# Second layer's value products in two passes instead of three, with the softmax sums taken from the exponential

## Chip, cores and metric

One core of a Trainium2 chip runs the whole program. The metric is device time in microseconds (us), the median of several runs. The profile is of one further execution, in which every instruction was recorded.

## The reference, cut to what matters

The reference is one step of a two-layer encoder over 512 new frames of one stream (the prompt) and 64 frames of a running stream with 256 cached frames (the sample). The first layer has differential attention, the second "forgetting" attention. Each layer ends with a gated feed-forward network. The change lies in the second layer's attention alone, with 16 heads of 64 columns:

```python
s = einsum('bqhd,bkhd->bhqk', q, k) * 64 ** -0.5
s = s + cq - ck                                   # forget terms of query and key
p = softmax(where(k_pos <= q_pos, s, -inf))
o = einsum('bhqk,bkhd->bqhd', p, v)
```

All inputs are float32, and the products need float32's precision.

## The kernel before, in words

**Split products.** TensorE's fast format for 4-byte numbers (F32R) keeps fewer bits than float32. So every operand is split into a high part (the number copied to that format by ScalarE) and a low part (the rest, by VectorE or GpSimd), and a product is made as high x high + high x low + low x high: three passes of matmuls into one PSUM tile. `slice_` (L583) does that for all weights: six matmuls of 288 columns for one slice of 128 rows.

**Slots.** The second layer works in 8 groups of 2 heads. A group's projections (K, Q and V) are 3 units of 8 slices, 24 slots. `fox_attention` of PE (L786) puts the attention of group a between the projection slices of group a + 1. For the last group the slices are those of the output projection (`wo`, L862). Each engine has a program of its own, written out for all slots, and a table gives the slot at which each operation stands (L73 to L83: F_SCORE, F_MAX, F_EXP and so on; slots above 23 lie in the next group). Each engine works its list in order, and semaphores hold it where an operand isn't ready.

**One head.** For each of 5 jobs (jj; the sample's is first, then the prompt's four blocks of 128 queries from the longest, of 512 keys, to the shortest, of 128), PE makes the scores in `sps` (L669), VectorE adds the mask and takes the row's extreme (`row_max`, L1545), ScalarE takes the exponential (`exps`, L1059), PE transposes it into `tps` (L689), ScalarE copies the high part to `pth` or `pts` (`take_p`, L1079) and VectorE makes the low part `ptl` (`p_lo`, L1591), which frees `tps` for the next transposes. The next job's transposes wait for that.

**Value products and division.** The weights of the value product are 128 columns wide: 64 of V's high part and 64 of ones (`vh2`), or 64 of V's low part and 64 of zeros (`vl2`). So the output `ops` holds the product in one half of its partitions and the softmax's sum, repeated 64 times, in the other. `pv_sample` (L721) makes 6 matmuls (3 key blocks; one of 128 and one of 64 columns each), `pv_prompt` (L741) 12 (blocks of 512, 384, 256 and 128 columns, 3 passes each). `recip` (L1108) and `log_sample` (L1100) take the logarithm of the sums and exp(-x) of it on ScalarE into `rec`, `scale_o` (L1611) multiplies on VectorE, and `fox_o_hi` (L1116) and `fox_o_lo` (L1618) split the result for the output projection. `ops` is one tile: the next value product or V transposition waits until `scale_o` has read it.

**SP's queue.** SP issues all transfers in order (L491 to L525): a weight unit in each 8 slots (slot 6 of 8), the copies of K and Q between partition halves (`copy_k`, `copy_q`), loads of cached K and V, and stores of new K and V.

Of the kernel before, what the change touches and what calls it, by code (L numbers as in the profile page):

```python
# [12 lines left out]
P = 128  # L13
# [5 lines left out]
TQ = SEQ + P  # L19
# [59 lines left out]
F_K, F_Q, F_V = (9, 17, 24)  # L79
F_K_HI, F_K_LO, F_AUG = (11, 23), (14, 24), (17, 21)  # L80
F_Q_HI, F_Q_LO = (20, 21)
F_W_LO, F_SPLIT = (3, 1)
F_DUP_K, F_DUP_Q = (15, 25), 21  # L83
# [3 lines left out]
NORM_AT = 2  # L87
MASK_AT, MASK_COLS = 3 * P, 6 * P
# [55 lines left out]
def encoder(nc, w_units, w_forget, x_in, small, cst, cst16, rope_tab, k_past, v_past, f_past,  # L144
# [3 lines left out]
    with ExitStack() as ctx:  # L148
# [86 lines left out]
        vh2 = place("vh2", [P, 7, 4, 64], F32R)  # L235
        vl2 = place("vl2", [P, 7, 4, 64], F32R)
# [123 lines left out]
        den_logs = sem("den_logs")  # L360
# [20 lines left out]
        def v_parts(L, v, v2):  # L381
# [3 lines left out]
            return ((v2[:, 0:4, 0:4:3, :], tps.rearrange("p b (h n) -> p b h n", h=2)),  # L385
                    (v2[:, 4, 0:4:3, :], ops[:, 0:P].rearrange("p (h n) -> p h n", h=2)),
                    (v2[:, 5:7, 0:4:3, :], v_raw.rearrange("p b (h n) -> p b h n", h=2)))
# [12 lines left out]

        block = ctx.enter_context(nc.Block())
# [3 lines left out]
        def _(sp):  # L405
# [67 lines left out]

            def copy_q(g):
# [16 lines left out]
            def second_layer():  # L491
# [13 lines left out]
                for t in range(SLOTS * G + WO_ALL):  # L505
# [11 lines left out]
                    for a in range(G):  # L517
                        for h in range(2):
                            if t - SLOTS * a == F_DUP_K[h]:
                                copy_k(a, h)  # L520
# [61 lines left out]
        def _(pe):  # L582
# [134 lines left out]
            def head_cols(v, blk, h):  # L717

                return v[:, blk, 2 * h:2 * h + 2, :].rearrange("p x n -> p (x n)")

            def pv_sample(L, a, h):  # L721
# [3 lines left out]
                if L == FOX:  # L725
                    if some(a * 2 + h):
                        pe.wait_ge(o_scaled, val(a * 2 + h))
                    if a.c == 0 and h == 0:
                        pe.wait_ge(fox_set, 4)
                elif later(a):  # L730
                    pe.wait_ge(oln_done, val(a))
                hi, lo = (vh, vl) if L == DIFF else (vh2, vl2)
                wide, narrow = (hi, 2 * NEW), (lo, NEW)
# [1246 lines left out]
```

## Time and profile before

| | |
|---|---|
| median of 3 runs | 1491.17 us (1490.64 to 1492.05) |
| the profiled execution | 1489.46 us |
| its span, first to last instruction | 1487.6 us |
| PE busy | 1457.0 us, 98% |
| DVE busy | 592.3 us, 40% |
| ACT busy | 620.7 us, 42% |
| POOL busy | 445.7 us, 30% |
| transfers | 135.04 MB, mean 91 GB/s |

PE is TensorE, DVE VectorE, ACT ScalarE, POOL GpSimd, SPq the queue of the sync engine. Matmuls overlap one another, so what a matmul costs is read from the start of one to the start of the next rather than from its duration. The second layer's attention runs from about 760 to 1023 us of the span.

### The profile page before, as it was taken

What the parts mean: (1) busy time and instruction counts of PE and PEld (TensorE: products, weight loads), DVE (VectorE), ACT (ScalarE), POOL (GpSimd) and SP (SyncE); (2) the same over time, 40 slices, a digit from 0 to 9 for tenths busy, and PEclk for the clock granted to TensorE, in tenths of its full rate; (3) what the DMA queues carried; (4) which work ended last, traced back from release to release, by engine and by line L of the source; (5) the groups of instructions that cost most, each with busy time, mean ns of one, the idle gap of its engine ahead of it and who ended that gap; (6) DMA issues with size and microseconds to landing.
All of it is one profiled execution on the core that took longest, in us unless ns stands there. A gap on an engine that the chain in (4) does not pass through costs nothing.

```text
span 1487.6 us, 28062 instructions
## 1 busy us (share of the span) xinstructions
PE 1457.0 (98%) x10763; PEld 1417.0 (95%) x10763; DVE 592.3 (40%) x1205; ACT 620.7 (42%) x1043; POOL 445.7 (30%) x221
## 2 busy tenths in 40 slices
PE   7999999999999999999989999999999999999997
PEld 7889989999999999999989999999999999999997
DVE  6788777441111111111266666663511111111113
ACT  5566666442222222222246767764522222222121
POOL 0000001344444444433500000013444444444332
PEclk9999999999999999999999999999999999999999
DMA  5333333222222222222333343332222222222322
GB/s 192 120 103 104 105 101 91 72 71 85 85 79 77 84 85 82 79 92 78 110 110 88 87 115 100 99 84 71 71 85 85 82 76 82 85 81 79 87 84 89
DMA packets 48763, 135.04 MB, mean 91 GB/s; under 512 B 6752, under 2 KB 13280, under 8 KB 48688
## 3 DMA queue, kind: packets, MB, share of 16 engines
q1 hardware_dynamic: 48688, 134.02, 29.8%
q8 instruction: 49, 0.80, 0.2%
q14 instruction: 26, 0.21, 0.0%
HBM read 111.19 MB, written 11.83 MB: 83 GB/s over the span
## 4 chain that ended last, share of the span: by engine, by line
PE 88%; DVE 4%; ACT 3%; issue 2%; DMA 1%; POOL 1%; SPq 0%; DVEq 0%; ACTq 0%
PE ps L590 76%; PE ops L749 3%; PE tps L701 2%; PE sps L664 2%; PE ps L631 1%; ACT w_hi L957 1%; PE sps L687 1%; PE sps L681 1%; DVE qa L1541 1%; DVE pr L1560 1%; POOL w_lo L1344 0%; PE ops L756 0%; PE tps L714 0%; PE sps L827 0%; PE ops L737 0%
## 5 line engine op out<-in xcount | busy, mean ns | idle before, releaser
L1344 POOL TENSOR_TENSOR w_lo<-w_raw,w_hi 128x1024 fp32r<-128x1024 f32 (+1 forms) x159 | 373.6, 2350 | 1013.0 <-ACT w_hi L957 1011.5
L590 PE MATMUL ps<-xh,w_hi 128*128 128x288 f32 x2160 | 475.1, 301 | 10.1 <-issue 4.4
L590 PE MATMUL ps<-xh,w_lo 128*128 128x288 f32 x2160 | 462.8, 296 | 0.0
L590 PE MATMUL ps<-xl,w_hi 128*128 128x288 f32 x2160 | 462.4, 296 | 0.0
L957 ACT ACTIVATE w_hi<-w_raw 128x1024 fp32r<-128x1024 f32 (+1 forms) x199 | 207.6, 1043 | 447.0 <-PE ps L590 443.7
L590 PEld LDWEIGHTS ps<-xh,w_hi 128*128 128x128 f32 x2160 | 345.9, 189 | 20.6 <-issue 16.7
L590 PEld LDWEIGHTS ps<-xh,w_lo 128*128 128x128 f32 x2160 | 348.0, 189 | 0.0
L590 PEld LDWEIGHTS ps<-xl,w_hi 128*128 128x128 f32 x2160 | 348.0, 189 | 0.0
L590 PE MATMUL ps<-hh,w_hi 128*128 128x288 f32 x660 | 141.4, 294 | 0.0
L590 PE MATMUL ps<-hl,w_hi 128*128 128x288 f32 x660 | 140.4, 294 | 0.0
L590 PE MATMUL ps<-hh,w_lo 128*128 128x288 f32 x660 | 140.1, 293 | 0.0
L1464 DVE TENSOR_TENSOR uf<-ps,rs 128x576 f32<-128x576 f32 x44 | 33.3, 757 | 232.7 <-PE ps L590 232.7
L1859 DVE TENSOR_TENSOR hl<-hf,hh 128x576 f32 (+1 forms) x44 | 33.3, 758 | 228.7 <-ACT hh L1311 228.7
L1458 DVE TENSOR_TENSOR xT<-ps,xT 128x576 f32<-128x576 f32 (+1 forms) x43 | 32.5, 755 | 211.8 <-PE ps L590 211.5
L590 PEld LDWEIGHTS ps<-hl,w_hi 128*128 128x128 f32 x660 | 106.2, 187 | 0.0
L590 PEld LDWEIGHTS ps<-hh,w_lo 128*128 128x128 f32 x660 | 105.4, 188 | 0.0
L590 PEld LDWEIGHTS ps<-hh,w_hi 128*128 128x128 f32 x660 | 105.4, 188 | 0.0
L1311 ACT ACTIVATE hh<-hf 128x576 f32 (+1 forms) x44 | 30.2, 686 | 178.4 <-POOL hf L1400 178.4
L1560 DVE CUSTOM_DVE_ANT_0 pr<-sps,smalls 128x384 f32<-128x384 f32 (+3 forms) x160 | 75.3, 500 | 43.6 <-PE sps L687 24.1
L1599 DVE TENSOR_TENSOR ptl<-tps,pth 128x512 fp32r<-128x512 f32 (+1 forms) x96 | 47.0, 490 | 57.1 <-ACT pth L1091 56.8
L1400 POOL TENSOR_TENSOR hf<-sg,uf 128x576 f32<-128x576 f32 x44 | 62.8, 1428 | 0.0
L1065 ACT ACTIVATE pr<-pr,nmax 128x384 f32<-128x384 f32 (+3 forms) x80 | 45.0, 564 | 37.3 <-DVE nmax L1560 37.3
(211 smaller groups left out, 1705.8 us busy)
## 6 DMA issues: line engine op xcount, KB each, us to landing
w_raw<-w_units SPq DMA_DIRECT2D x184, 512.0 KB, 3.6
w_raw<-w_units SPq DMA_DIRECT2D x16, 384.0 KB, 3.0
qsw<-qsin SPq DMA_DIRECT2D x64, 72.0 KB, 2.0
ka<-ka SPq DMA_DIRECT2D x16, 224.0 KB, 4.5
xT<-x_in SPq DMA_DIRECT2D x8, 288.0 KB, 5.2
dk_out<-kf SPq DMA_DIRECT2D x8, 288.0 KB, 2.5
dv_out<-vf SPq DMA_DIRECT2D x8, 288.0 KB, 2.2
fk_out<-kf SPq DMA_DIRECT2D x8, 288.0 KB, 2.2
```

The source lines that it names most:

```text
L590: mm = nc.tensor.matmul(out[:, half, :], w[:, k, :], rhs[:, kt, half * HALF:(half + 1) * HALF], start=start and w is w_hi[slot] and rhs is ...
L749: mm = nc.tensor.matmul(ops[:, P * j:SEQ], w, p[:, j, P * j:SEQ], start=j == 0 and v is hi and p is pth, stop=j == 3 and v is lo)
L957: nc.scalar.activation(w_hi[slot][:, 0:kts, :], w_raw[slot][:, 0:kts, :], ACT.Copy).then_inc(w_hi_done, 1)
L1065: nc.scalar.activation(pr[:, slot, 0:width(i)], pr[:, slot, 0:width(i)], ACT.Exp, scale=-1.0, bias=nmax[:, slot:slot + 1], accum_out=den[: ...
L1311: nc.scalar.activation(at(hh, jt), hf[:], ACT.Copy).then_inc(hh_done, 1)
L1344: nc.gpsimd.tensor_tensor(w_lo[slot][:, 0:kts, :], w_raw[slot][:, 0:kts, :], w_hi[slot][:, 0:kts, :].bitcast(F32), ALU.subtract).then_inc( ...
L1400: nc.gpsimd.tensor_tensor(hf[:], sg[:], uf[:], ALU.mult).then_inc(hf_done, 1)
L1458: tt(halves(at(xT, k)), proj(n.c % 2), halves(at(xT, k)), ALU.add).then_inc(ps_read, 1)
L1464: tt(halves(dst), proj(n.c % 2) if src is None else src, halves(scale), ALU.mult).then_inc(ps_read, 1)
L1560: nc.vector.tensor_tensor_reduce(pr[:, slot, 0:width(i)], sps[:, jj % 2, 0:width(i)], mask[:, first:first + width(i)], -1.0, 3.0e38, ALU.a ...
L1599: tt(dst, src, hi.bitcast(F32), ALU.subtract).then_inc(pt_lo, 1)
L1859: tt(at(hl, jt), hf[:], at(hh, jt).bitcast(F32), ALU.subtract).then_inc(hl_done, 1)
```

## The change

V's high and low part now lie side by side in one tile `vv`, so that one matmul with the 128 columns [V high, V low] gives both products, one in each half of the partitions. Only the passes over P's high and P's low part are left. The ones are gone, and with them the sums. The exponential adds its row up (`accum_out`) into `dens`, and VectorE takes the reciprocal of five columns at a time (`make_share`). The result lies with queries across partitions, and it's needed with queries along the row, the same in 64 partitions. So one transfer writes it element by element to a row in HBM (`send_share`), and a second reads that row into 64 partitions (`fetch_share`). ScalarE copies the one half of `ops` to the partitions of the other (`move_prompt`, `move_sample`; before: logarithm, then exp), VectorE adds the halves (`join_o`) and multiplies by the fetched shares (`weigh_o`). The slot tables change in places. The two POOL memsets of ones and zeros go.

```diff
-F_SCORE, F_MAX, F_EXP = (3, 4, 5, 7, 7, 13, 13, 15, 18, 18), (1, 5, 5, 9, 9, 12, 14, 15, 18, 18), (2, 5, 6, 9, 9, 14, 14, 15, 18, 19)
-F_TURN, F_TAKE_P, F_P_LO = (5, 7, 9, 11, 13, 15, 17, 18, 21, 24), (5, 7, 9, 11, 13, 15, 16, 18, 21, 22), (6, 7, 9, 11, 12, 15, 16, 18, 21, 22)
-F_VT, F_TAKE_V, F_V_LO = (4, 1, 3)
-F_PVS, F_TAKE_S, F_SUM_S = (7, 17), (8, 19), (7, 19)
-F_PVP, F_SCALE_O, F_O_HI, F_O_LO = (15, 25), (16, 25), (17, 25), (17, 29)
-F_LN_S, F_RECIP = (10, 21), (15, 24)
+F_SCORE, F_MAX, F_EXP = (2, 5, 5, 7, 7, 13, 13, 15, 18, 18), (1, 5, 5, 7, 9, 13, 14, 15, 17, 18), (2, 5, 6, 8, 9, 13, 14, 15, 18, 18)
+F_TURN, F_TAKE_P, F_P_LO = (5, 7, 9, 12, 13, 15, 17, 18, 21, 24), (5, 8, 9, 10, 13, 15, 16, 18, 21, 22), (6, 7, 9, 9, 13, 15, 16, 18, 21, 22)
+F_VT, F_TAKE_V, F_V_LO = (3, 3, 3)
+F_PVS, F_TAKE_S, F_SUM_S = (9, 17), (9, 20), (9, 20)
+F_PVP, F_SCALE_O, F_O_HI, F_O_LO = (15, 25), (16, 25), (17, 28), (18, 28)
+F_LN_S, F_RECIP = (12, 21), (15, 25)
-F_DUP_K, F_DUP_Q = (15, 25), 21
+F_DUP_K, F_DUP_Q = (16, 25), 21
+F_SHARE, F_WEIGH, F_SEND, F_FETCH = (11, 20), (16, 27), (11, 18), (16, 24)
...
-        vh2 = place("vh2", [P, 7, 4, 64], F32R)
-        vl2 = place("vl2", [P, 7, 4, 64], F32R)
+        vv = place("vv", [P, 7, 4, 64], F32R)
+        share = place("share", [P, T])
+        dens = place("dens", [P, 2, 2, 8])
+        shares = place("shares", [P, 2, 2, 8])
...
+            def send_share(a, h):
+                sp.wait_ge(share_made, 2 * a + h + 1)
+                sp.dma_start(share_rows[2 * a + h].rearrange("(i p) -> p i", p=P), shares[:, a % 2, h, 0:5],
+                             allow_slow_non_contiguous=True).then_inc(share_out, 16)
+
+            def fetch_share(a, h):
+                sp.wait_ge(share_out, 16 * (2 * a + h + 1))
+                if a > 0:
+                    sp.wait_ge(o_joined, 2 * a + h - 1)
+                sp.dma_start(share[64 * h:64 * h + 64, :], share_rows[2 * a + h:2 * a + h + 1, 0:T].partition_broadcast(64)
+                             ).then_inc(share_in[h], 16)
...
                 if L == FOX:
                     if some(a * 2 + h):
                         pe.wait_ge(o_scaled, val(a * 2 + h))
-                    if a.c == 0 and h == 0:
-                        pe.wait_ge(fox_set, 4)
+                    for b in range(3):
+                        mm = nc.tensor.matmul(ops[:, 0:2 * NEW], head_cols(4 + b, h), pts[:, b, :], start=b == 0, stop=b == 2)
+                    mm.then_inc(pvs_done, 1)
+                    return
...
                 for j in range(4):
-                    for v, p in ((hi, pth), (hi, ptl), (lo, pth)):
+                    for v, p in ((vh, pth), (vh, ptl), (vl, pth)) if L == DIFF else ((vv, pth), (vv, ptl)):
...
                 else:
+                    if jj % 5 == 0 and a.c >= 2:
+                        act.wait_ge(share_made, 2 * (a.c - 2) + h + 1)
                     nc.scalar.activation(pr[:, slot, 0:width(i)], pr[:, slot, 0:width(i)], ACT.Exp, scale=-1.0,
-                                         bias=nmax[:, slot:slot + 1]).then_inc(exp_done, 1)
+                                         bias=nmax[:, slot:slot + 1], accum_out=dens[:, par, h, i:i + 1]
+                                         ).then_inc(exp_done, 1)
...
-            def recip(a, h):
+            def move_prompt(a, h):
                 act.wait_ge(pvp_done, G + i + 1)
-                nc.scalar.activation(rec[r, 0:SEQ], ops[o, :], ACT.Ln).then_inc(den_logs, 1)
-                act.wait_ge(den_logs, 2 * i + 2)
-                nc.scalar.activation(rec[r, :], rec[r, :], ACT.Exp, scale=-1.0).then_inc(rec_done, 1)
+                if a > 0:
+                    act.wait_ge(op_lo, i - 1)
+                nc.scalar.activation(rec[r, 0:SEQ], ops[o, :], ACT.Copy).then_inc(rec_done, 1)
...
-            def scale_o(a, h):
+            def join_o(a, h):
                 dve.wait_ge(rec_done, i + 1)
-                tt(rec[r, 0:SEQ], ops[r, :], rec[r, 0:SEQ], ALU.mult).then_inc(o_scaled, 1)
-                tt(rec[r, SEQ:T], osum[r, :], rec[r, SEQ:T], ALU.mult).then_inc(os_scaled, 1)
+                tt(rec[r, 0:SEQ], ops[r, :], rec[r, 0:SEQ], ALU.add).then_inc(o_scaled, 1)
+                dve.wait_ge(os_moved, i + 1)
+                tt(rec[r, SEQ:T], osum[r, :], rec[r, SEQ:T], ALU.add).then_inc(os_scaled, 1)
+
+            def weigh_o(a, h):
+                dve.wait_ge(share_in[h], 16 * (a + 1))
+                dve.wait_ge(o_scaled, i + 1)
+                dve.wait_ge(os_scaled, i + 1)
+                tt(rec[r, :], rec[r, :], share[r, :], ALU.mult).then_inc(o_joined, 1)
+
+            def make_share(a, par, h):
+                dve.wait_ge(exp_done, 10 * G + 10 * a + 5 * h + 5)
+                if a >= 2:
+                    dve.wait_ge(share_out, 16 * (2 * (a - 2) + h + 1))
+                nc.vector.reciprocal(shares[:, par, h, 0:5], dens[:, par, h, 0:5]).then_inc(share_made, 1)
...
-                for tile, value in ((vh2[:, :, 1:3, :], 1.0), (vl2[:, :, 1:3, :], 0.0)):
-                    nc.gpsimd.memset(tile.bitcast(F32), value).then_inc(fox_set, 2)
```

`fox_o_hi` waits for `o_joined` now. In SP's program `send_share` and `fetch_share` stand at their slots of the group, ahead of `copy_k` of the same slot. In VectorE's program `weigh_o` stands right behind `join_o` where both have slot 16.

## Rows read from the trace of the kernel before

**Rows 1.** The page, busy time of each engine.
```profile
PE 1457.0 (98%) x10763; PEld 1417.0 (95%) x10763; DVE 592.3 (40%) x1205; ACT 620.7 (42%) x1043; POOL 445.7 (30%) x221
```
**Rows 2.** Busy time by stretch: us, PE, PEld, DVE, ACT, POOL, clock, DMA, GB/s.
```profile
830.00:860.00 30.00, 29.58 (x218) 28.20 (x217) 20.92 (x49) 20.82 (x40) 2.40 (x1) 1.00 0.32 91
```
**Rows 3.** Waits, 750 to 1060 us: total us, times, longest.
```profile
PE tps L701 <- DVE vl L1589: 1.7, 7, 0.2
PE ops L749 <- DVE ptl L1599: 1.3, 7, 0.2
```
**Rows 4.** Timeline of PE, prompt value product: start, us, engine, line, operation.
```profile
780.25 0.40 PE L749 MATMUL ops<-pth,vh 128*128 128x512 f32 x1
...
782.10 0.39 PE L681 MATMUL sps<-ka,qa 128*128 128x384 f32 x1
```
**Rows 5.** Timeline of PE, sample value product of the third group.
```profile
835.91 0.31 PE L737 MATMUL ops<-pts,vh 128*128 128x128 f32 x1
836.05 0.24 PE L737 MATMUL ops<-pts,vl 128*128 128x64 f32 x1
836.13 0.30 PE L737 MATMUL ops<-pts,vh 128*128 128x128 f32 x1
...
836.61 0.48 PE L590 MATMUL ps<-xh,w_hi 128*128 128x288 f32 x2
```
**Rows 6.** Groups by line and form, ACT and DVE: busy us, mean ns | idle before.
```profile
L1065 ACT ACTIVATION_READ_ACCUMULATOR pr<-pr,nmax 128x1 f32 x80 | 15.0, 187 | 0.0
L1114 ACT ACTIVATE rec<-rec 64x576 f32<-64x576 f32 x16 | 10.9, 684 | 0.5
L1129 ACT ACTIVATE og<-ops 128x512 f32<-128x512 f32 x8 | 4.7, 592 | 1.1 <-PE ops L749 1.1
L1622 DVE TENSOR_TENSOR ol<-rec,oh 64x576 fp32r<-64x576 f32 x16 | 12.0, 752 | 1.4 <-ACT oh L1124 1.1
L1568 DVE RECIPROCAL rden<-den 128x1 f32<-128x1 f32 x40 | 6.3, 158 | 2.8 <-ACT pr L1065 2.8
```
**Rows 7.** Timeline of ACT, third group.
```profile
839.16 0.79 ACT L1069 ACTIVATE pr<-pr,nmax 128x256 f32<-128x256 f32 x2
...
846.53 0.59 ACT L1112 ACTIVATE rec<-ops 64x512 f32<-64x512 f32 x1 [1.46 <-PE ops L749]
...
849.40 0.60 ACT L1091 ACTIVATE pth<-tps 128x512 fp32r<-128x512 f32 x1 [0.70 <-PE tps L701]
...
852.85 0.80 ACT L1069 ACTIVATE pr<-pr,nmax 128x256 f32<-128x256 f32 x2
```
**Rows 8.** Timeline of DVE, third group.
```profile
848.50 0.67 DVE L1615 TENSOR_TENSOR rec<-ops,rec 64x512 f32<-64x512 f32 x1
849.10 0.21 DVE L1616 TENSOR_TENSOR rec<-osum,rec 64x64 f32<-64x64 f32 x1
850.03 0.69 DVE L1599 TENSOR_TENSOR ptl<-tps,pth 128x512 fp32r<-128x512 f32 x1 [0.72 <-ACT pth L1091]
...
853.33 1.22 DVE L1476 TENSOR_TENSOR w_lo<-w_raw,w_hi 128x1024 fp32r<-128x1024 f32 x1
```
**Rows 9.** Timeline of PE, the next transposes.
```profile
851.27 0.52 PE L701 MATMUL tps<-cstf,pr 128*128 128x128 f32 x3
```
**Rows 10.** DMA queue: packets, MB, share; then issues, KB each, us to landing.
```profile
q1 hardware_dynamic: 48688, 134.02, 29.8%
...
kf<-k_past SPq DMA_DIRECT2D x16, 128.0 KB, 3.5
...
half_sel<-cst SPq DMA_DIRECT2D x8, 1.0 KB, 2.8
...
lf_out<-lf SPq DMA_DIRECT2D x1, 36.0 KB, 1.6
```
**Rows 11.** Timeline of SP's queue, third group.
```profile
841.38 0.33 SPq L419 DMA_DIRECT2D w_raw<-w_units  x1
...
855.11 1.11 SPq L479 DMA_DIRECT2D qb<-qa  x2
```

More of the change, by code:

```diff
@@ L359, in encoder @@
         fox_set = sem("fox_set")
-        den_logs = sem("den_logs")
+        os_moved = sem("os_moved")
+        share_made = sem("share_made")
+        share_out = sem("share_out")
+        share_in = [sem(f"share_in{h}") for h in range(2)]
+        o_joined = sem("o_joined")
         rec_done = sem("rec_done")
@@ L378, in encoder, with v_parts @@
         y_done = sem("y_done")
-        def v_parts(L, v, v2):
+        def v_parts(L, v, low):
             if L == DIFF:
                 return ((v[:, 0:4, :], tps[:]), (v[:, 4, :], ops[:, 0:P]), (v[:, 5:7, :], v_raw[:]))
-            return ((v2[:, 0:4, 0:4:3, :], tps.rearrange("p b (h n) -> p b h n", h=2)),
-                    (v2[:, 4, 0:4:3, :], ops[:, 0:P].rearrange("p (h n) -> p h n", h=2)),
-                    (v2[:, 5:7, 0:4:3, :], v_raw.rearrange("p b (h n) -> p b h n", h=2)))
+            c = slice(1, 3) if low else slice(0, 4, 3)
+            return ((vv[:, 0:4, c, :], tps.rearrange("p b (h n) -> p b h n", h=2)),
+                    (vv[:, 4, c, :], ops[:, 0:P].rearrange("p (h n) -> p h n", h=2)),
+                    (vv[:, 5:7, c, :], v_raw.rearrange("p b (h n) -> p b h n", h=2)))
         def t_index(L, a, jj):
@@ L518, in second_layer @@
                         for h in range(2):
+                            if t - SLOTS * (a + 1) == F_SEND[h]:
+                                send_share(a, h)
+                            if t - SLOTS * (a + 1) == F_FETCH[h]:
+                                fetch_share(a, h)
                             if t - SLOTS * a == F_DUP_K[h]:
@@ L715, in transpose_v, with head_cols @@
                 nc.tensor.transpose(ops[:, 0:P], vf[:, SEQ:TQ], ident).then_inc(vt_done, 1)
[L717 to L719 removed]
+            def head_cols(blk, h):
+                return vv[:, blk, 2 * h:2 * h + 2, :].rearrange("p x n -> p (x n)")
             def pv_sample(L, a, h):
@@ L744, in pv_prompt @@
                 pe.wait_ge(os_taken, val(v_index(L, a, h) + 1))
-                hi, lo = (vh, vl) if L == DIFF else (vh2, vl2)
                 for j in range(4):
-                    for v, p in ((hi, pth), (hi, ptl), (lo, pth)):
-                        w = v[:, j, :] if L == DIFF else head_cols(v, j, h)
-                        mm = nc.tensor.matmul(ops[:, P * j:SEQ], w, p[:, j, P * j:SEQ],
-                                              start=j == 0 and v is hi and p is pth, stop=j == 3 and v is lo)
+                    for v, p in ((vh, pth), (vh, ptl), (vl, pth)) if L == DIFF else ((vv, pth), (vv, ptl)):
+                        w = v[:, j, :] if L == DIFF else head_cols(j, h)
+                        mm = nc.tensor.matmul(ops[:, P * j:SEQ], w, p[:, j, P * j:SEQ], start=j == 0 and v is not vl and p is pth,
+                                              stop=j == 3 and (v is vl or v is vv and p is ptl))
                 mm.then_inc(pvp_done, 1)
@@ L1053, in take_v @@
                     act.wait_ge(pvp_done, val(v_index(L, a, 0)))
-                for b, (dst, src) in enumerate(v_parts(L, vh, vh2)):
+                for b, (dst, src) in enumerate(v_parts(L, vh, False)):
                     if b == 2:
@@ L1704, in fox_attention @@
                         if s == F_SCALE_O[h]:
-                            scale_o(a, h)
+                            join_o(a, h)
+                        if s == F_WEIGH[h]:
+                            weigh_o(a, h)
+                        if s == F_SHARE[h]:
+                            make_share(a, par, h)
                         if s == F_O_LO[h]:
```

35 lines of the change are left out of this document (17 added, 18 removed).

## The prediction

> **What bounds the kernel.** I read the page's busy times first: PE is busy in 98% of the span and each other engine in under half [rows 1]. An average says nothing of one stage, so next the busy time of 30 us inside the second layer's attention, at the full granted clock (2.4 GHz): PE 29.58, DVE 20.92, ACT 20.82 us [rows 2]. Then who PE waits for there: the longest sums that a DVE operation causes are 1.7 and 1.3 us in all, each 7 waits of at most 0.2 us [rows 3]. So this stage is the length of PE's work, and DVE and ACT have a third of it spare, if what is added doesn't come at a wrong moment. Since PE is in order and dense, a matmul taken out is worth the distance from its start to the next one's start.
>
> **What PE loses: the prompt's third pass.** 12 matmuls of `pv_prompt` take from 780.25 to 782.10 us, where the next operation starts: 1.85 us [rows 4]. The three passes have the same shapes (512, 384, 256, 128 columns), so one is a third, 0.617 us. It goes for 2 heads of 8 groups, 16 times: 9.9 us.
>
> **The sample's product.** Six matmuls take from 835.91 to 836.61, 0.70 us; one of 128 columns is 0.14 before the next, the first one of 64 columns 0.08 [rows 5]. Three of 128 columns stay. At 0.14 each they take 0.42 and 0.28 us is saved; if each costs what the average of the six is (0.70 / 6 = 0.117), 0.35 us are saved; the lowest price in sight is the 0.08 of the small one, 0.24, which saves 0.46. I take the middle one: 16 x 0.35 = 5.6 us, with ends 4.5 and 7.4.
>
> The Trainium skill (TensorE: Matmul & The Clock Gate, section "Wait — 56ns, not 53.3ns?") has another price: a matmul costs its columns at 2.4 GHz and some 2.5 ns. By that the prompt's pass would be 0.54 us, and the sample's saving (576 columns before, 384 after) 0.09 us: 10.1 us in all. The prompt's row agrees within some 15%; the sample's doesn't, 0.70 us against 0.26 by the rule. Such a low gain is one of the rivals below, with the price of my rows.
>
> **ACT.** Out: the exp over 576 columns, 16 x 0.684 = 10.9 us. The logarithm (0.59 us) becomes a copy, and a copy of 512 columns out of `ops` takes the same 0.592 [rows 6, 7]. In: the reading of the accumulator behind each exponential, 0.187 us [rows 6], for 80 exponentials: 15.0 us. Together +4.1 us over 8 groups of some 32 us, 0.5 us a group. Cover: ACT's idle third [rows 2]. If it had none, it would be 4 us. More of interest is that each exponential is done 0.19 us later for the transposes; at present no transposition waits for an exponential (the waits that there are stand in [rows 3]), so I cost it at nothing.
>
> **DVE.** The two multiplications become two additions of the same shapes (0.67 and 0.21 us [rows 8]): nothing. In: one multiplication of 64x576 from SBUF, by the nearest row 0.752 us, and one reciprocal, 0.158 us for one column and hardly more for five [rows 6]. 16 x 0.91 = 14.6 us, nearly 2 us a group, from 20.9 to some 22.7 in 30 us. Again in idle time, provided the operands are there.
>
> **The tile `ops`** gets free earlier: product 0.6 us shorter, and no exp of 0.68 between the copy and DVE's operation. A gain only where PE waited for that; it doesn't [rows 3], so nothing. **POOL's** two memsets and PE's one wait for them go: nothing, as POOL has no part in the stage's end.
>
> **The way of the sums.** This is the only new wait on a shared engine, so I followed its times, on the third group's first head. The last two exponentials end at 839.16 + 0.79 = 839.95 [rows 7], with two reads of the accumulator 840.3; reciprocal 840.5. Then `send_share`: 640 separate elements of 4 bytes to HBM. No row shows such a transfer. The lower bound is the quickest landing, 1.6 us (`lf_out`). The nearest in size of its pieces is 2.8 us (16 rows of `half_sel`, 1 KB). The upper bound: all of the queue's packets, mostly of kilobytes, cost on average 0.298 x 1487.6 x 16 / 48688 = 0.146 us on one of 16 engines; 40 of them on each are 5.8 us, and with the 1.6 us 7.4 [rows 10]. I take 2.8: landed at 843.3. `fetch_share`, 64 rows and 147 KB out of HBM, is like the load of cached K, 3.5 us (lower bound 2.8): 846.8.
>
> When does DVE need it? ACT now starts on `ops` at 846.53 [rows 7], after the change 0.6 us sooner, 845.9; copy to 846.5, two additions of 0.67 and 0.21 and the hand-overs: 847.6. So the share is there 0.8 us before the multiplication can start, which then ends at 848.4. Behind it in DVE's list stands the low part of the next transposed block, which has to wait for ACT in any case: it starts at 850.03, behind a copy from 849.40 [rows 7, 8], 0.6 us sooner after the change, 849.4. So there is a further 1.0 us of cover; the share costs nothing up to a landing at 848.65, 1.85 us after my estimate. For the second head the table leaves 7 slots between reciprocal and multiplication instead of 5, and though DVE splits weights from 853.33 to 854.55, just ahead of the reciprocal [rows 8], it is the looser one of the two.
>
> **SP's queue.** Two waits come before other transfers. Behind `send_share` of the first head stand a store, the load of cached V and the weight unit of 841.38 [rows 11]; SP passes it at 840.5, so nothing is late for the weights. `fetch_share` holds `copy_k` up to some 843.3, which the next group's scores need, 10 slots (over 10 us) later. `send_share` of the second head waits until some 854.7, and the `copy_q` behind it waits for its own operand up to 855.11 anyway [rows 11]. `fetch_share` of the second head then holds one copy and a store for 2 or 3 us; a weight unit issued at slot 22 is first split 11 slots later. All costed at nothing; if the cover of a weight unit were gone, PE would wait for it in every group.
>
> **The sum.** Gain 9.9 + 5.6 = 15.5 us. Against it some small waits: PE is ahead of the others by nearly 1 us a group more, and the 14 waits of 3.0 us in sum [rows 3] may grow by half: 1.5 us. Net 14.0. The profiled execution took 1489.46 us around a span of 1487.6; it should come to some 1475.5. The median of the runs is 1.7 us above that execution, so 1491.2 - 14.0 = 1477.2. I give 1477.0.
>
> **Rivals.**
>
> 1. *Gain partly given back.* The 0.187 us behind each exponential and 2 us more of DVE a group delay low parts on which transposes wait. If half of the 80 reads came to stand in PE's way, 7.5 us are lost: 1484.5. The low gain (sample product saves the 0.09 or little more) without any waits gives 1491.2 - 9.9 - 1.4 = 1479.9, and with them up to 1486. For it: rows of 0.2 us waits show that some low parts are just in time. Against: none of these waits names an exponential. Chance 0.15 for 1480 to 1488.
>
> 2. *DVE stands at the multiplication for the share: slower.* Place: `weigh_o` of the first head, at slot 16; behind it the low part of the 512 block, without which the transposes of 851.27 [rows 9] don't start. It decides from a landing after 848.65. At the upper bound (send 7.4, fetch 3.5 us) the share lands at 840.5 + 10.9 = 851.4, 2.75 us late, 8 times: 22 us, less the 15.5: 1497.7. Even with before is at 1.9 us late. For it: two transfers one behind the other, the fetch standing behind a 512 KB weight unit and a store in the same queue, and 640 pieces. Against: even the sum of the nearest rows leaves 1.85 us. The Trainium skill (DMA: Bandwidth & Descriptors, section "Rules for kernel authors") speaks against this edit: a strided last dimension becomes one descriptor per element, and it advises to rearrange. It gives no price for 640 of them; if the rearranged pattern's 19-fold cost, given there for transposes by plain transfers, held for the 1.6 us, this would be far beyond the upper bound, and no row here shows it. Chance 0.08.
>
> 3. *No change.* The removed matmuls' time comes back as waits, since PE and the others go in step: about 1491. Against it the spare third [rows 2]. Chance 0.04.
>
> That the change doesn't do what it says: the sums could be read before they are complete or the pass could stay; the matmul count excludes the latter, and the former would change no time. No chance of its own.
>
> **Chances and range.** Forecast 0.73, for 1473 to 1480: ends from the sample term (4.5 to 7.4 instead of 5.6, prompt's third 0.58 to 0.65) and waits of 0 to 3 us. Rival 1 0.15, rival 2 0.08, rival 3 0.04. The range of 8 in 10 is the forecast's own, stretched into rival 1: 1473 to 1484. A measurement of this kernel tells differences from 0.2%, 3 us. Faster by more than that: forecast and rival 1, 0.88. Within: rival 3 and a little of 2, 0.05. Slower: 0.07.
>
> **What the changed profile would show.** PE has 3 x 16 + 4 x 16 = 112 matmuls less (10651), `pv_prompt` takes 1.23 us instead of 1.85, the sample's product 0.35 instead of 0.70. The waits of DVE name the share's transfer for at most a few us in all, and PE's waits stay under some 6 us in the stage. ACT gains 80 accumulator reads of 0.19 us. Wrong would be: a send that lands after 5 us or more, a multiplication in `weigh_o` with a DMA as releaser and over 1 us each time, PE idle before transposes in each group, or a stage whose PE work shrinks by under 12 us.

## The result, and the profile after

Slower by 8%: 1613.61 us is the median of the changed kernel (1612.60 to 1616.90, 4 runs), against 1490.91 us for the kernel before, measured beside it (4 runs). The ratio is 1.0829, 95% interval 1.0815 to 1.0842. The prediction said 1477.0 us, range 1473 to 1484. The profiled execution has a span of 1610.8 us.

The page, busy time of each engine and the granted clock in 40 slices; the first line answers to [rows 1]:

```profile
PE 1476.1 (92%) x10651; PEld 1435.4 (89%) x10651; DVE 607.3 (38%) x1237; ACT 616.5 (38%) x1107; POOL 443.0 (28%) x219
...
PEclk9999999999999999999889888888899999999999
```

PE has the 112 matmuls less that were foretold (10651), and yet it is busy 19.1 us longer than before. Its idle time, span less busy, went from 1487.6 - 1457.0 = 30.6 us to 134.7. So two things are to be explained: 104 us of waiting, and busy time that grew although work went. Who waits for what, in the list of waits over the whole run (total us, times, longest) for PE, DVE and SP's queue; the first line answers to the waits for a low part in [rows 3]:

```profile
PE tps L728 <- DVE ptl L1625: 74.3, 8, 9.8
PE sps L714 <- DMA qb<-qa: 26.1, 8, 4.9
...
DVE rec L1651 <- DMA share<-share_rows: 96.1, 16, 10.2
...
SPq L494 <- DMA share_rows<-shares: 129.6, 15, 10.3
```

DVE's multiplication in `weigh_o` stands for the share in all 16 heads, up to 10.2 us. PE's transposes wait for the low part behind it once in each of 8 groups, 9.3 us on average. A second wait, of 26.1 us, is for the copies of the new queries. Both lead back to SP's queue, shown here from the timeline (start us, duration, line, operation) for both heads of one group:

```profile
873.79 0.38 SPq L486 DMA_DIRECT2D share_rows<-shares  x1
874.22 0.52 SPq L448 DMA_DIRECT2D fk_out<-kf  x1
...
883.68 0.47 SPq L494 DMA_DIRECT2D share<-share_rows  x1
...
894.22 0.38 SPq L486 DMA_DIRECT2D share_rows<-shares  x1
894.65 1.43 SPq L502 DMA_DIRECT2D qb<-qa  x2
...
904.19 0.46 SPq L494 DMA_DIRECT2D share<-share_rows  x1
```

The fetch may only go out when the send has landed: 9.9 and 10.0 us after it here, 9.6 to 12.6 us over the 16 heads. My estimate was 2.8, my upper bound 7.4. What is issued behind the send lands late too: `fk_out` took 12.0 us (median) where it took 2.2.

The trace also shows what the DMA engines do in that time. For each of the 16 sends some 670 packets of 4 bytes start within the first 3 us, 7 ns each in the median. After that little moves until the send has landed (columns of [rows 2]):

```profile
877.80:883.60 5.80, 3.71 (x31) 3.56 (x29) 1.60 (x5) 2.79 (x6) 0.00 (x0) 1.00 0.43 25
```

That is 25 GB/s at a DMA share of 0.43, where the stretch in [rows 2] has 91 GB/s at 0.32: the packets of the other transfers last long and carry little. From 4 us after the issue to 1 us before the fetch it is 18 to 34 GB/s for each of the 16 sends. So the 10 us don't go into starting one piece after another; they pass between the start of the pieces and their landing.

DVE and PE at the end of this group's wait (timeline; in brackets the idle time before and its releaser); then two pairs of the same matmuls from an undisturbed stretch; then the busy time by stretch with the columns of [rows 2]:

```profile
889.26 0.75 DVE L1651 TENSOR_TENSOR rec<-rec,share 64x576 f32<-64x576 f32 x1 [9.71 <-DMA share<-share_rows]
889.93 0.67 DVE L1625 TENSOR_TENSOR ptl<-tps,pth 128x512 fp32r<-128x512 f32 x1
...
890.75 0.87 PE L728 MATMUL tps<-cstf,pr 128*128 128x128 f32 x3 [9.24 <-DVE ptl L1625]
...
892.39 0.68 PE L617 MATMUL ps<-xh,w_lo 128*128 128x288 f32 x2
892.87 0.68 PE L617 MATMUL ps<-xh,w_hi 128*128 128x288 f32 x2
```

```profile
779.56 0.43 PE L617 MATMUL ps<-xl,w_hi 128*128 128x288 f32 x2
779.83 0.42 PE L617 MATMUL ps<-xh,w_lo 128*128 128x288 f32 x2
```

```profile
836.00:848.00 12.00, 4.10 (x18) 4.13 (x19) 5.03 (x12) 4.34 (x10) 0.00 (x0) 0.58 0.33 73
...
884.00:910.00 26.00, 15.44 (x92) 14.53 (x92) 13.21 (x26) 11.03 (x23) 0.00 (x0) 0.80 0.68 102
...
891.00:893.00 2.00, 2.00 (x10) 2.00 (x10) 2.00 (x8) 1.83 (x6) 0.00 (x0) 0.50 0.02 4
```

After PE had stood for 9.24 us, two matmuls of 288 columns take 0.48 us from start to start, where the same pair took 0.27 us at 779.56. From 891 to 893 us the granted clock is 0.50, so 1.2 instead of 2.4 GHz, called the half clock below; over the two longer stretches its mean is 0.58 and 0.80. This is the busy time that grew: the removed products are worth 15.4 us (below), so 19.1 + 15.4 = 34.5 us were added. The trace lets it be counted in a second way. Over the whole run PE is busy for some 76 us while the granted clock is 0.50, in the kernel before for 3. Of the 0.48 us for a pair 0.21 are added by the low clock, and of the 73 us more at this clock the same share is 32 us, an estimate.

One group, from the first head's sample product to the same in the next group, takes 46 to 48 us instead of 32.1.

### The profile page after: what moved, and what is told of

The parts are those of the page before. It is cut to its first block, busy times and chain, and to the rows that moved or that the text cites. A ratio compares the mean times of both kernels' runs of the same rounds, so it can differ in the third digit from the quotient of the medians.

```text
span 1610.8 us, 28016 instructions
## 1 busy us (share of the span) xinstructions
PE 1476.1 (92%) x10651; PEld 1435.4 (89%) x10651; DVE 607.3 (38%) x1237; ACT 616.5 (38%) x1107; POOL 443.0 (28%) x219
## 4 chain that ended last, share of the span: by engine, by line
PE 75%; DMA 15%; DVE 4%; issue 2%; ACT 2%; POOL 1%; SPq 1%; DVEq 0%; ACTq 0%
PE ps L617 68%; DMA share_rows<-shares 8%; DMA share<-share_rows 3%; DMA qb<-qa 2%; PE tps L728 2%; PE sps L691 1%; PE ops L775 1%; PE ps L658 1%; DVE ptl L1625 1%; POOL w_lo L1372 0%; PE ops L782 0%; PE tps L741 0%; PE sps L853 0%; DVE pr L1586 0%; PE sps L714 0%
## 5 line engine op out<-in xcount | busy, mean ns | idle before, releaser
L617 PE MATMUL ps<-xh,w_hi 128*128 128x288 f32 x2160 | 485.0, 307 | 8.9 <-issue 3.9
L617 PE MATMUL ps<-xl,w_hi 128*128 128x288 f32 x2160 | 470.1, 300 | 0.0
L617 PE MATMUL ps<-xh,w_lo 128*128 128x288 f32 x2160 | 469.9, 300 | 0.0
L617 PEld LDWEIGHTS ps<-xh,w_hi 128*128 128x128 f32 x2160 | 354.5, 194 | 18.6 <-issue 16.6
L617 PEld LDWEIGHTS ps<-xl,w_hi 128*128 128x128 f32 x2160 | 355.9, 193 | 0.0
L617 PEld LDWEIGHTS ps<-xh,w_lo 128*128 128x128 f32 x2160 | 355.2, 193 | 0.0
L728 PE MATMUL tps<-cstf,pr 128*128 128x128 f32 x312 | 59.2, 293 | 78.7 <-DVE ptl L1625 74.3
L728 PEld LDWEIGHTS tps<-cstf,pr 128*128 128x128 f32 x312 | 39.2, 148 | 85.2 <-issue 75.2
```

What stands on the lines that cost most here:

```text
L617: mm = nc.tensor.matmul(out[:, half, :], w[:, k, :], rhs[:, kt, half * HALF:(half + 1) * HALF], start=start and w is w_hi[slot] and rhs is ...
L728: mm = nc.tensor.transpose(tps[:, b, :], pr[:, slot, P * b:P * b + P], ident)
```

## The experiments

"Before" is the kernel before, measured beside each experiment: 1490.4 to 1490.6 us each time. "Send to fetch" is the distance of the two issues on SP's queue. The fetch also has a slot of its own, so for quick sends this is an upper bound.

**1. No transfers.** The share tile is filled with ones by POOL, so the division is left out:

```diff
-                            if t - SLOTS * (a + 1) == F_SEND[h]:
-                                send_share(a, h)
-                            if t - SLOTS * (a + 1) == F_FETCH[h]:
-                                fetch_share(a, h)
+                nc.gpsimd.memset(share[:], 1.0).then_inc(share_set, 1)
```

> The changed kernel without both transfers: the multiplication takes a tile of ones set once, so the output isn't divided by the sums; exponential, reciprocal, moves and slot tables stay. Theory A (the transfers by way of HBM alone cost the 123 us, and the rest of the forecast stands): PE idle of the stage back to that of before, no stretch at the low clock, two-pass products worth 13 to 16 us: 1475 to 1480 us. Theory B (the accumulator reads, the extra VectorE work or the new slot tables also hold PE): between 1485 and 1560 us, with PE waits on ptl that don't name a transfer.

1481.1 us, ratio 0.9939 (0.9923 to 0.9956), 1 us above theory A's range. All else of the change is a gain; the way of the sums is the whole loss, 1613.6 - 1481.1 = 132.5 us. Added up over 16 heads, from first matmul to the next operation, the prompt products went from 30.54 to 20.48 us and the sample products from 11.16 to 5.86: 15.4 us (the 15.2 us in an expectation below is the same sum from rows rounded to 0.01 us). Of this 9.3 us arrive in the time. The largest wait that was added stands in the list:

```profile
PE ops L772 <- DVE ptl L1624: 4.0, 7, 0.6
```

**2. The send in 128 pieces of 20 bytes.** Each partition writes its five shares side by side, so they reach the tokens in another order:

```diff
-share_rows[2 * a + h].rearrange("(i p) -> p i", p=P), shares[:, a % 2, h, 0:5], allow_slow_non_contiguous=True
+share_rows[2 * a + h].rearrange("(p i) -> p i", p=P), shares[:, a % 2, h, 0:5]
```

> The send writes each partition's five values side by side, 128 pieces of 20 bytes instead of 640 of 4 (the shares come back in another order, so the output is wrong in its scaling). Theory A (the engines write small pieces to HBM one after the other, about 10 us / 40 = 0.25 us each): 8 pieces on an engine, landing in 2 to 4 us; the kernel within 1475 to 1500 us. Theory B (a write to HBM with a second transfer behind it is slow as such, whatever the pieces): still 8 to 10 us from send to fetch, and over 1580 us.

1490.81 us (one run); send to fetch 1.8 to 3.4 us. The form of the write is the cause of the 10 us, and not the way to HBM as such. But for the order in which the shares arrive nothing else differs from the change, so the form alone is worth 1613.6 - 1490.8 = 122.8 of the 132.5 us. The share is still late at times, and the whole gain of the products is gone again:

```profile
DVE rec L1651 <- DMA share<-share_rows: 15.5, 10, 3.4
```

**3. Fewer columns.** The send writes 5, 4, 3, 2, 1, 5, 3 and 1 columns in the eight groups, and the fetch reads a row of constants (no division):

```diff
+                n = (5, 4, 3, 2, 1, 5, 3, 1)[a]
-share_rows[2 * a + h].rearrange("(i p) -> p i", p=P), shares[:, a % 2, h, 0:5]
+share_rows[2 * a + h, 0:n * P].rearrange("(i p) -> p i", p=P), shares[:, a % 2, h, 0:n]
```

> Groups 0 to 7 send 5, 4, 3, 2, 1, 5, 3, 1 of the five columns (640, 512, 384, 256, 128, 640, 384, 128 pieces of 4 bytes); the fetch reads a constant row, so the output isn't the reference's. Theory A (a price by piece): the time from send to fetch is a straight line in the number of pieces, about 1.6 us + 0.21 us for each piece on an engine: 10, 8.3, 6.6, 5, 3.3, 10, 6.6, 3.3 us. Theory B (a fixed price for such a pattern, as in its preparation): 9 to 10 us for each group. Rival C (writes to neighbouring addresses hinder each other): not a line, steeper with more columns.

1599.5 us (one run). Send to fetch, first head: 10.9, 9.8, 9.6, 9.4, 8.4, 10.9, 9.6 and 8.1 us. A fifth of the pieces takes nearly as long as all. So a price per piece, on which my upper bound was built, is refuted. Theory B, one price for such a pattern, fits these numbers best; what about the pattern is dear is open until experiments 4 and 5. A column is 128 neighbouring words in HBM, and five columns take only 2 to 3 us longer than one.

**4. The same 640 pieces, written into SBUF** (again with constants fetched):

```diff
-share_rows[2 * a + h].rearrange("(i p) -> p i", p=P), shares[:, a % 2, h, 0:5]
+spread[:, 0:10:2], shares[:, a % 2, h, 0:5]
```

> The send's 640 pieces of 4 bytes go into SBUF (every second word of a small tile) instead of HBM, and the fetch reads a constant row of HBM; the output isn't the reference's. Theory A (it is the small write to HBM that is slow): 2 to 3.5 us from send to fetch, kernel at 1475 to 1495 us. Theory B (640 separate pieces are slow wherever they go, in making or moving them): 8 to 10 us and over 1580 us.

1492.46 us (one run); send to fetch 2.2 to 3.6 us. So 640 pieces of 4 bytes aren't slow as such; in HBM, side by side, they are.

**5. Eight forms of a write to HBM,** one per group, with constant data and no division:

```diff
+                n, step = ((5, 0), (1, 1), (1, 16), (1, 128), (16, 16), (8, 8), (2, 2), (1, 8))[a]
+                    dst = forms[2 * a + h, 0:P * step].rearrange("(p n) -> p n", n=step)[:, 0:n]
+                    sp.dma_start(dst, pieces[:, 0:n], allow_slow_non_contiguous=True).then_inc(share_out, 16)
```

> Edit: the send writes a constant tile in a form of its own in each of the 8 groups, and the fetch reads a constant row, so the division is left out. Forms by group: 640 pieces of 4 bytes as in the change; 128 pieces of 4 bytes side by side; 128 of 4 bytes each 64 bytes apart; 128 of 4 bytes each 512 bytes apart; 128 of 64 bytes side by side; 128 of 32 bytes side by side; 128 of 8 bytes side by side; 128 of 4 bytes each 32 bytes apart. Read as the time from send to fetch on the sync engine's queue. Theory A (writes of a few bytes that fall beside each other in HBM are made one after the other): about 9 to 10 us in the groups 0 and 1, 5 to 9 in group 6 (8 bytes), under 3.5 in groups 3, 4 and 5, and the spacing at which it falls tells the size of the stretch that is held. Theory B (each write of 4 bytes to HBM is slow, wherever it falls): 8 us or more in groups 1, 2, 3 and 7 alike, under 3.5 in 4 and 5.

1516.53 us (one run).

| pieces | send to fetch, us, heads 0 and 1 |
|---|---|
| 640 of 4 B, five columns, as in the change | 10.8, 11.7 |
| 128 of 4 B, side by side | 9.0, 7.9 |
| 128 of 4 B, 64 B apart | 1.9, 2.7 |
| 128 of 4 B, 512 B apart | 3.0, 2.3 |
| 128 of 64 B, side by side | 3.2, 2.2 |
| 128 of 32 B, side by side | 1.9, 2.2 |
| 128 of 8 B, side by side | 3.8, 4.3 |
| 128 of 4 B, 32 B apart | 3.2, 2.7 |

The timeline of SP's queue, second and third form:

```profile
847.02 0.33 SPq L493 DMA_DIRECT2D forms<-pieces  x1
...
854.88 0.49 SPq L503 DMA_DIRECT2D share<-cst  x1
...
872.00 0.33 SPq L493 DMA_DIRECT2D forms<-pieces  x1
...
873.88 0.49 SPq L503 DMA_DIRECT2D share<-cst  x1
```

The same 128 pieces of 4 bytes are about four times quicker when they lie 64 bytes apart, and 32 bytes are enough. Pieces of 8 bytes side by side take half as long as those of 4, less than the 5 to 9 us that I expected. So writes are slow when they start 4 bytes apart, half as slow at 8 bytes, and quick at 20 (experiment 2) and 32 bytes. No run has a distance between 8 and 20 bytes. The Trainium skill (DMA: Bandwidth & Descriptors, section "Specifications") says that below 512 B a transfer does a read-modify-write. That alone doesn't tell the slow forms here from the quick ones, since all pieces are below 512 B. If its read-modify-writes are what is made one after the other here, then only where pieces share such a stretch; no run here shows the mechanism itself.

**6. Slow send, late multiplication.** The first idea for a repair without touching the transfer (of the slot tables, here and below, only what changes is shown):

```diff
-F_O_HI, F_O_LO = (17, 28), (18, 28)
+F_O_HI, F_O_LO = (24, 36), (24, 36)
-F_WEIGH = (16, 27)
+F_WEIGH = (23, 35)
```

> Edit: the slow send stays as it is in the change; only the multiplication by the shares (and the products of osum after it) stand 7 to 8 slots later, some 7 us behind their old place. Theory A (most of the loss is VectorE standing at the multiplication, in front of the masking of the next product's tiles): the wait of PE's prompt transposes for ptl falls from 74 us to under 15 in sum, the half clock goes with it (PE busy from 1476 to about 1455), and the time falls to 1495 to 1525, what is left being the new queries' copies that stand behind the send on the sync engine's queue (26 us in the change). Rival (the time of the multiplication does not matter, since the queue's block alone sets the group): 1580 us or more, with qb and fk waits of 80 us.

1542.84 us (one run): above the 1495 to 1525 that I had expected, below the rival's 1580. Waits:

```profile
PE sps L714 <- DMA qb<-qa: 22.1, 8, 4.9
PE ops L775 <- DVE ptl L1625: 11.0, 13, 2.2
PE sps L708 <- DMA ka<-ka: 8.2, 2, 4.5
...
PE tps L728 <- DVE ptl L1625: 2.8, 4, 1.5
```

The wait behind the multiplication went from 74.3 to 2.8 us, and the time fell by 71 us: PE is idle 57 us less (77.2 instead of 134.7) and busy 12 us less. It isn't one for one, since the waits in the second and third line here are new. What stays are mostly transfers that are issued while the send runs, 22.1 + 8.2 us, and PE's busy time is 1463.8 us, above the 1455 that I had expected and 21 above that of experiment 8.

**7. As 6, with the send in ScalarE's queue:**

```diff
-                sp.dma_start(share_rows[2 * a + h]...
+                nc.scalar.dma_start(share_rows[2 * a + h]...
```

> Edit: as the late multiplication, and the slow send is issued from ScalarE's queue, so that no copy of queries or keys stands behind it in its queue. Theory A (what stands behind the send waits because of the order within one queue): fk_out and qb land within 2 to 4 us again, no wait of PE for qb over 1 us, 1482 to 1495 us. Rival (the send holds the 16 DMA engines themselves): qb, fk_out and also the caches' loads take 8 us or more while it runs, whatever the queue, and the time is within 5 us of the late multiplication alone, or above it.

On ScalarE the send stands at slots 13 and 22 (on SP at 11 and 18), and each head has a semaphore of its own.

1533.4 us (one run), 9.4 us below experiment 6: neither theory A's 1482 to 1495 nor the rival's 5 us. The DMA issues of the page (KB each, median us to landing), first two of the kernel before, then of this run:

```profile
fk_out<-kf SPq DMA_DIRECT2D x8, 288.0 KB, 2.2
qb<-qa SPq DMA_DIRECT2D x16, 144.0 KB, 2.5
```

```profile
fk_out<-kf SPq DMA_DIRECT2D x8, 288.0 KB, 2.2
qb<-qa SPq DMA_DIRECT2D x16, 144.0 KB, 8.7
...
share_rows<-shares ACTq DMA_DIRECT2D x16, 2.5 KB, 10.1
```

`qb` is issued while a send runs (865.74, send 865.23) and lands late, 8.7 us in the median, from a queue of its own; `fk_out` now goes out when none runs, and takes 2.2. The weight units of 512 KB show the same: the 8 that SP issues beside a send of ScalarE's queue land after 10.6 to 12.0 us, the others after 3.6 in the median. My theory of the order within one queue is refuted: the send holds up whatever kind of transfer runs beside it. This agrees with the Trainium skill (DMA: Bandwidth & Descriptors, section "Issuing engines are not separate DMA queues"), by which all queues end on the same 16 DMA engines. The interleaving between queues of which that section speaks did not help `qb` here. Why the time still fell by 9 us was not tried; in the attention 8 weight units lie beside a send now, in experiment 6 it was 16.

**8. Turned rows.** DVE turns the sums in blocks of 32 by 32 ahead of the reciprocal, and each head's shares leave as 4 transfers of 8 rows of 128 bytes. The multiplication stands 4 slots later, and the first head's fetch 2 slots sooner.

```diff
-                nc.vector.reciprocal(shares[:, par, h, 0:5], dens[:, par, h, 0:5]).then_inc(share_made, 1)
+                nc.vector.transpose(turned[:], dens[:, par, h, :]).then_inc(turn_done, 1)
+                dve.wait_ge(turn_done, 2 * a + h + 1)
+                nc.vector.reciprocal(shares[:, par, h, :], turned[:]).then_inc(share_made, 1)
+                for q in range(4):
+                    sp.dma_start(share_rows[2 * a + h][:, 32 * q:32 * q + 32], shares[32 * q:32 * q + 8, a % 2, h, :]
+                                 ).then_inc(share_out, 16)
...
-F_O_HI, F_O_LO, F_WEIGH, F_FETCH = (17, 28), (18, 28), (16, 27), (16, 24)
+F_O_HI, F_O_LO, F_WEIGH, F_FETCH = (21, 32), (23, 33), (20, 31), (14, 24)
```

> Edit: the exponential's sums are turned on VectorE (32 columns by 32 partitions) before the reciprocal, so that each head's shares leave SBUF as 4 transfers of 8 rows of 128 bytes instead of 640 pieces of 4 bytes; the multiplication and the two products of osum stand 4 slots later. The output is the whole one. Theory A (the cost of the change is the time that neighbouring 4-byte writes to HBM take): from the send to the fetch on the sync engine's queue 1.8 to 3.5 us instead of 9.1 to 12, the wait of the prompt product's first transposes for ptl back to under 12 us in sum instead of 74, no half clock in the middle of the groups, and 1478 to 1484 us: the 15.2 us of products are kept, 4 to 6 are given back to small waits as without any transfers (1481.1). Theory B (any way to HBM and back within a group costs about 9 us, whatever the pieces): 1550 us or more. The kernel before ran in 1490.4.

1479.65 us, ratio 0.9927 (0.9910 to 0.9943), with the whole computation: 0.7% faster than the kernel before, and 1.5 us below experiment 1, which has no transfers at all but the early slots. The page's busy times and the timeline of SP's queue:

```profile
PE 1443.1 (98%) x10651; PEld 1404.2 (95%) x10651; DVE 613.8 (42%) x1253; ACT 614.3 (42%) x1107; POOL 446.1 (30%) x220
```

```profile
841.75 1.30 SPq L490 DMA_DIRECT2D share_rows<-shares  x4
...
844.53 0.47 SPq L498 DMA_DIRECT2D share<-share_rows  x1
```

Send to fetch 2.8 us, which was my estimate; over the 16 heads 2.2 to 4.6. And with the same 10651 matmuls PE is busy 1476.1 - 1443.1 = 33 us less than in the change, while its busy time at a granted clock of 0.50 goes from 76 to 7 us: another reading of the price of the half clock.

**9. The third pass put back** into 8 (the low part of the exponentials is counted twice):

```diff
-... else ((vv, pth), (vv, ptl)):
+... else ((vv, pth), (vv, ptl), (vv, ptl)):
```

> Edit: as the turned rows (1479.65), with a third pass put back into the second layer's prompt product (the low part of the exponentials a second time, so the output counts it twice): 4 matmuls more for each of 16 products. Theory (a pass is worth its distance on PE, 0.617 us by the trace of before, and 10.0 us in sum by the products of the run without transfers): 1487.5 to 1490, the products 1.85 us each again. Rival (the pass removed is partly worth nothing, because PE waits for the low parts in its place): under 1485, with the waits of PE for ptl (4.0 and 0.9 us) gone. Smaller ones of these waits may go in either case.

1486.9 us (10 runs), ratio to before 0.9978 (0.9968 to 0.9988). It costs 7.3 us, just under the 8 to 10 I expected and above the rival's 5. The two intervals together leave some 4 to 10 us, so the times alone don't exclude the rival; the traces speak against it. Inside the attention the price is nearly whole: a group takes 31.5 us instead of 30.4, 1.1 us, where the two products grew by 10.2 / 8 = 1.27; the waits for ptl (4.2 and 0.8 us) didn't go.

**10. Quick send, the change's own slots** for the multiplication:

```diff
-F_O_HI, F_O_LO, F_WEIGH = (21, 32), (23, 33), (20, 31)
+F_O_HI, F_O_LO, F_WEIGH = (17, 28), (18, 28), (16, 27)
```

> Edit: as the turned rows, with the multiplication and osum's two parts at the slots of the change (16 and 17 for the first head instead of 20, 21 and 23). Theory (only the send's length made the early place of the multiplication dear; now the share lands some 8 us after the send starts, by the trace of the turned rows at about 849.2 in a group where slot 16 comes at some 848.6): the multiplication waits 0 to 2 us in each group, PE's prompt transposes wait up to 12 us in sum for ptl, 1480 to 1492. Rival (4 slots more make no difference): 1479 to 1481, tps never waits for ptl by more than 1 us in sum.

1503.82 us, ratio 1.0107 (1.0080 to 1.0133): 1% slower than before even with a quick send, and 12 us above my upper end. Waits, then the timeline of ACT and DVE around the first head's share:

```profile
PE tps L732 <- DVE ptl L1633: 16.9, 8, 2.8
...
DVE rec L1659 <- DMA share<-share_rows: 22.7, 10, 3.3
```

```profile
844.58 0.19 ACT L1103 ACTIVATION_READ_ACCUMULATOR pr<-pr,nmax 128x1 f32 x1
...
847.26 0.42 DVE L1633 TENSOR_TENSOR ptl<-tps,pth 128x256 fp32r<-128x256 f32 x1 [2.28 <-ACT pth L1126]
...
847.98 0.35 DVE L1670 RECIPROCAL shares<-turned 128x32 f32<-128x32 f32 x1
...
852.90 0.67 DVE L1649 TENSOR_TENSOR rec<-ops,rec 64x512 f32<-64x512 f32 x1
...
856.15 0.75 DVE L1659 TENSOR_TENSOR rec<-rec,share 64x576 f32<-64x576 f32 x1 [2.44 <-DMA share<-share_rows]
```

The sums are complete at 844.77. The reciprocal ends at 848.33, since it stands in DVE's order behind a low part that waits 2.28 us for ACT. In the change itself the same low part waits 2.27 us ahead of the reciprocal. The share is there at 856.15, 7.8 us after the reciprocal; DVE could have used it at 853.71.

**11. As 8, with the first head's multiplication 3 slots later still:**

```diff
-F_O_HI, F_O_LO, F_WEIGH = (21, 32), (23, 33), (20, 31)
+F_O_HI, F_O_LO, F_WEIGH = (24, 32), (24, 33), (23, 31)
```

> Edit: as the turned rows, with the first head's multiplication 3 slots later still (23), out of the stretch in which the second head's last low parts are made. Theory (the wait of PE's second prompt product for the last ptl, 0.6 us in each group, 4.0 in sum, comes of DVE being dense between slots 19 and 22): the wait falls under 1.5 us and the time to 1475 to 1478. Rival (the two low parts of the queries stand in the way and not the multiplication): the wait stays at 3 us or more and the time within 1.5 us of 1479.65.

1484.92 us, ratio 0.9966 (0.9952 to 0.9980), 5 us worse than 8.

```profile
PE tps L745 <- DVE rec L1649: 8.9, 7, 1.4
...
PE ops L779 <- DVE ptl L1633: 1.4, 7, 0.2
```

The old wait fell to 1.4 us, as the theory had it, but a new one of 8.9 us took its place: DVE now comes late to the second head's output in `ops`, for which the next group's transposes of V wait. The gain that the theory hung on it didn't come.

**12. As 10, the first head's reciprocal one slot sooner,** ahead of that low part:

```diff
-F_SHARE = (11, 20); F_P_LO[3] = 9; F_SUM_S = (9, 20)
+F_SHARE = (10, 20); F_P_LO[3] = 10; F_SUM_S = (10, 20)
```

> Edit: as the turned rows at the change's own slots for the multiplication (1503.82), with the first head's reciprocal one slot sooner on VectorE, ahead of the low part of the 256-column block and of osum, on which it does not depend. In the trace without this edit the last read of the sums ends at 844.77, VectorE stands from 844.90 to 847.26 for ScalarE's copy of that block, and only then come the turning and the reciprocal (848.33); the multiplication then stands 2.44 us for the share. Theory (the place of the reciprocal in VectorE's list is a term of its own, as dear as the send's form): the reciprocal ends 2.4 to 2.7 us sooner, the waits of the multiplication for the share fall from 22.7 us in sum to under 6, the waits of PE's transposes for ptl from 16.9 to under 5, and the time to 1479 to 1486. Rival (the share's fetch is held by what stands ahead of it in the sync engine's queue, so a sooner send lands no sooner at the multiplication): the waits stay above 12 us and the time above 1495.

1487.65 us (10 runs), ratio 0.9978 (0.9969 to 0.9988): 16 us better than 10 for three operations at other slots, just short of the 1486 I expected. The waits of the multiplication fell to 9.1 us, not under 6; those of PE's transposes for ptl to 1.9 us. The timeline of SP's queue, then DVE's wait for the share:

```profile
838.98 1.30 SPq L490 DMA_DIRECT2D share_rows<-shares  x4
...
842.80 0.47 SPq L498 DMA_DIRECT2D share<-share_rows  x1
```

```profile
DVE rec L1659 <- DMA share<-share_rows: 9.1, 12, 1.9
```

The send now starts 7.4 us before DVE's work on `ops` (846.35), in 10 it was 4.5 (848.36 and 852.90), so 2.8 us were won. One was lost again on SP's queue, where send to fetch is 3.8 instead of 2.8 us. The rival was right in this small part, and in this group only: in six of the other seven the first head's distance is 2.8 us.

## Why the prediction was wrong

Rival 2 took place, in its mechanism and at its spot, the low part behind the multiplication in `weigh_o`. It stood at 1497.7 us with a chance of 0.08; both price and chance were far too low. In the order of the prediction's steps:

**The products: right.** 15.5 us foretold, 15.4 measured in experiment 1 (prompt 10.1 for 9.9; sample 5.3 for 5.6). The price by columns that I had set beside it, 0.26 us for a sample product before, is not what the rows show, 0.70 before and 0.37 after.

**Small waits, ACT and DVE: nearly right.** With the way of the sums taken out it is 1481.1, inside the range and 4 us above the forecast; the largest wait is the 4.0 us for ptl, where 1.5 us had been allowed for all of them.

**The send: wrong, the step that decided.** 2.8 us from the row with the nearest size of piece, 7.4 as an upper bound from the queue's average per packet; measured 9.6 to 12.6. The bound rested on packets of kilobytes and on counting, and the cost hardly depends on the count (experiment 3) nor on the pieces' size alone (4), but on their being neighbours in HBM (5). In time: experiment 2 differs from the change by the form of the send alone, 1613.6 - 1490.8 = 123 us (one run). Experiment 10, with the whole computation and a turn on DVE ahead of the send, gives 1613.6 - 1503.8 = 110 us. By the profiles of 10 and of the change PE is idle for 134.7 instead of 1499.1 - 1450.5 = 48.6 us, 86 us more, and busy for 1476.1 instead of 1450.5, 26 us more. The idle part is DVE standing at the multiplication and transfers beside the send (74.3 and 26.1 us of PE's waits in the change); the busy part is the half clock behind PE's long waits, which the sum had not at all.

**The start of the way: wrong, and independent of the send.** I let the reciprocal run at 840.5, as soon as the sums were complete. Its place in DVE's written order is behind a low part that stands for ACT, and it begins 3.2 us after the last sum in experiment 10. The trace of before had the sign of it, an idle of 1.15 us ahead of the same low part:

```profile
841.01 0.42 DVE L1599 TENSOR_TENSOR ptl<-tps,pth 128x256 fp32r<-128x256 f32 x1 [1.15 <-ACT pth L1091]
```

I had read where the multiplication comes, and not what stands ahead of the reciprocal. Experiment 12 shows that this alone makes 16 us with a quick send.

**The fetch: too low.** 3.5 us taken from the load of cached K; its median in experiment 8 was 4.7. From the reciprocal's end to the share are 7.8 us in 10, where 6.3 were summed. And from the reciprocal's end to the point at which DVE could multiply are 5.4 us (848.33 to 853.71), where I had 7.1 (840.5 to 847.6). That is 1.5 and 1.7 us, together 3.2: my 0.8 us early became 2.4 us late, and 2.44 stands in the row. Of the further 1.0 us of cover behind the multiplication 0.4 was left, as PE stood 2.00 us in that group. So even at my own price for the send the forecast should have been rival 2's. Experiment 2 says so too: with a send of 1.8 to 3.4 us in the change's own order the time is 1490.8, no gain at all.

**SP's queue: wrong.** `copy_q` was costed at nothing, because it waits for its own operand anyway. I had asked when it is issued, and not what its landing takes beside a running send: 8.7 instead of 2.5 us in experiment 7. In the change PE waits 26.1 us for it.

What stays open: what happens to neighbouring words between the start of their packets (within 3 us) and their landing, and how exactly the send holds back transfers from another queue. The half clock was not tried by itself; its price is the difference of busy time between kernels with the same matmuls, and the count of busy time at the low granted clock comes near it (32 us).

## What to carry to other kernels

Before a column of single words goes from SBUF to HBM, turn it on chip: a 0.20 us turn on DVE made a way of 10 us one of 2.8, and together with a later multiplication the change became a gain. When a value is sent round by DMA, write down both ends in the engines' own lists, what stands ahead of its making and what stands behind its use; here either end was worth as much as the whole gain (16 us in experiment 12, 24 between 10 and 8). And a long wait of PE can cost more than its length: behind the waits of some 9 us here the granted clock was 0.50, which made PE's busy time some 34 us longer.

## What was not expected of the hardware

- 128 writes of 4 bytes to neighbouring words of HBM took 7.9 to 10.4 us (experiments 3 and 5), the same 32 or 64 bytes apart 1.9 to 3.2, and 640 of them in five columns 9.6 to 12.6 in the change.
- All packets of such a write started within 3 us; until it landed, the 16 DMA engines moved 18 to 34 GB/s, in the kernel before 91 (830 to 860 us).
- Pieces of 20 and of 32 bytes side by side were as quick as larger ones: 1.8 to 3.4 us.
- While such a write ran, a copy of 144 KB from another queue took 8.7 us instead of 2.5, and a load of 512 KB 10.6 to 12.0 instead of 3.6.
- A reciprocal of 128x32 took 0.35 us and one of 128x5 0.18.
